# Window attention with the oldest key tile of all eight heads in a unit of its own

## The reference, cut to what matters

```python
s = jnp.einsum('bntgrd,bnsgd->bngrts', q, k).astype(jnp.float32) * scale
dist = q_pos[:, :, None] - k_pos[:, None, :]
bias = rel_bias[rel_bucket(dist)]...
valid = (dist >= 0) & (dist < WINDOW) & (k_pos[:, None, :] >= 0)     # WINDOW = 512
p = masked_softmax(s + bias[None], valid[None, :, None, None])
return jnp.einsum('bngrts,bnsgd->bntgrd', p.astype(v.dtype), v)
```

## Time and profile before

| | |
|---|---|
| median of 3 runs | 1117.7 us (1116.35 to 1119.99) |
| the profiled execution | 1116.44 us |
| its span | 1114.3 us |
| TensorE busy | 1074.0 us, 96% |
| VectorE, ScalarE, GpSimd busy | 618.8, 359.9, 88.9 us |
| mean granted TensorE clock | 0.987 |

### The profile page before, as it was taken

The page is one execution under the profiler, slowest core; times in us unless marked ns, Lnnn a source line. Parts: engine busy times, 40 slices in busy tenths (PEclk is TensorE's granted clock), DMA queues, the critical chain, the costliest instruction groups (busy, mean ns, idle before and its releaser), DMA issues.

```text
span 1114.3 us, 22552 instructions
## 1 busy us (share of the span) xinstructions
PE 1074.0 (96%) x8364; PEld 768.0 (69%) x8364; DVE 618.8 (56%) x1613; ACT 359.9 (32%) x875; POOL 88.9 (8%) x192
## 2 busy tenths in 40 slices
PE   6899999999999999998999999999999999999997
PEld 2455599998886687777876766764545476777775
DVE  0635323463423477767676666742324588888883
ACT  0422001121112475545455555631112123333330
POOL 0210100110000111100101010011000200000000
PEclk8999999999999999999999999999999999999997
DMA  9933260011006230000000000005794367788881
GB/s 350 314 114 95 79 204 2 16 35 56 1 1 123 55 106 1 1 1 1 2 1 2 1 1 1 1 1 120 162 316 150 135 220 267 268 273 290 276 216 57
DMA packets 96612, 120.25 MB, mean 108 GB/s; under 512 B 31569, under 2 KB 65380, under 8 KB 95480
## 3 DMA queue, kind: packets, MB, share of 16 engines
q1 hardware_dynamic: 96504, 118.81, 34.5%
HBM read 104.41 MB, written 14.36 MB: 107 GB/s over the span
## 4 chain that ended last, share of the span: by engine, by line
PE 84%; issue 8%; SPq 3%; DVE 3%; ACT 1%; DMA 1%; POOL 0%; ACTq 0%; POOLq 0%; DVEq 0%
PE PS L548 19%; PE PS L2047 10%; PE PS L1736 7%; PE PS L1714 7%; PE PS L1690 6%; PE PS L540 4%; PE PS L2549 3%; PE PS L1677 3%; PE PS L1711 3%; PE PS L2511 2%; PE PS L2562 2%; PE PS L1686 2%; PE PS L1242 1%; PE PS L647 1%; SPq L376 1%
## 5 line engine op out<-in xcount | busy, mean ns | idle before, releaser
L548 PE MATMUL PS<-AR 128*128 128x256 f32 (+2 forms) x896 | 219.7, 403 | 0.0
L548 PEld LDWEIGHTS PS<-AR 128*128 128x128 f32 x896 | 167.8, 190 | 45.2 <-issue 6.2
L1736 PE MATMUL PS<-CA,AR 128*128 128x128 f32 x704 | 112.2, 282 | 0.2 <-ACT AR L1790 0.2
L2047 PE MATMUL PS<-AR 128*128 128x512 f32 x256 | 112.3, 592 | 0.0
L962 DVE TENSOR_TENSOR AR<-PS,AR 128x256 f32<-128x256 f32 (+2 forms) x80 | 36.2, 453 | 134.0 <-PE PS L548 133.9
L1806 ACT ACTIVATE AR<-PS 128x512 f32<-128x512 f32 (+1 forms) x108 | 58.2, 546 | 138.6 <-PE PS L1736 137.9
L1736 PEld LDWEIGHTS PS<-CA,AR 128*128 128x128 f32 x704 | 77.9, 144 | 34.9 <-issue 25.8
L1714 PE MATMUL PS<-AR 128*128 128x65 f32 (+1 forms) x768 | 99.6, 270 | 0.0
L1714 PEld LDWEIGHTS PS<-AR 128*128 128x128 f32 x768 | 94.2, 192 | 0.2
L1790 ACT ACTIVATE AR<-PS,SM_ 128x512 f32<-128x512 f32 (+4 forms) x208 | 83.6, 475 | 17.8 <-DVE SM_ L1871 10.2
L2047 PEld LDWEIGHTS PS<-AR 128*128 128x128 f32 x256 | 47.5, 190 | 54.0 <-issue 54.0
(11 more groups left out here) (360 smaller groups left out, 1574.3 us busy)
## 6 DMA issues: line engine op xcount, KB each, us to landing
AR<-in_cache_nsa SPq DMA_DIRECT2D x128, 256.0 KB, 4.7
AR<-in_cache_mla SPq DMA_DIRECT2D x128, 96.0 KB, 3.6
AR<-in_x_prompt SPq DMA_DIRECT2D x16, 512.0 KB, 4.6
AR<-in_w_ada SPq DMA_DIRECT2D x3, 2048.0 KB, 11.8
AR<-in_w_in SPq DMA_DIRECT2D x6, 1024.0 KB, 8.7
AR<-in_w_ada SPq DMA_DIRECT2D x8, 512.0 KB, 4.4
AR<-in_w_out SPq DMA_DIRECT2D x4, 1024.0 KB, 11.4
AR<-in_w_out SPq DMA_DIRECT2D x2, 2048.0 KB, 17.5
```

The costliest lines, as they stand in the source:

```text
L548: mm = pe.matmul(bank[:, 0:WIDE[g]], tokens[:, k, :], w, start=(fresh and k == 0), stop=(last and k == 3), skip_group_check=True)
L1736: mm = pe.transpose(PS[:, 4 + c % 2, P * (t - t0):P * (t - t0) + P], tile(u, t), ident)
L2047: mm = pe.matmul(PS[0:n, 2 + 2 * (m % 2) + c, :], YTO[m % 2][:, f, 0:n], weights[:, f, 512 * c:512 * c + 512], start=(f == 0), stop=(f == 7))
```

## The change

- For each block i >= 4 a new unit `old` comes between the select and the window units. It takes one score slot (1024 columns) and holds the scores of the oldest key tile for all eight heads, 128 columns each. VectorE adds `wmask` and writes the 1024 results to `BTX[:, :, 256:384]` in SBUF, which frees the slot (`s_old`), and takes eight minima into `EM`. The unit has no exponentials and no chunks of its own.
- A window unit of blocks 4 to 7 then has four key tiles in PSUM and takes one slot. VectorE takes the minimum over the far 256 columns of both heads at once, takes the minimum of that with `EM`, and handles the nearest 256 columns per head (384 before). Its last two exponentials read `BTX` instead of PSUM. It still has ten tiles in three chunks: the first is copied by ScalarE, the second and third by VectorE, as before.
- `early` now speaks of units with exponentials, so the exponentials of a window unit stand ahead of the copies of the window unit before it.
- Window groups of block 4 are crossed and turned back too.
- The scores of a one-slot unit after a window unit with one slot wait for two exponentials of it (`MANY`, not `TWO`); after a two-slot unit they wait for all four.
- GpSimd no longer copies the mask into `BTX`.

The diff, with one line around each edit:

```diff
 NM2 = small(2)
+EM = small(8)
 NM = small(16).rearrange("p (s g) -> p s g", s=2)
...
     pool.wait_ge(s_fl, 4)
-    for h in range(H):
-        pool.tensor_copy(BTX[:, h, 256:384], wmask).then_inc(s_btw, 1)
     pool.memset(VM[:, :, :, 128:129], 2.0).then_inc(s_one, 1)
...
     nb = 1 if kind == "cmp" else i + 1 - k0
+    if kind == "win" and i >= 4:
+        UNITS.append(("old", i, 0, [(r, g) for r in range(R) for g in range(G)], k0, 1, len(GROUPS)))
     for half in range(2):
...
 for u, (kind, i, half, heads, k0, nb, og) in enumerate(UNITS):
-    if nb > 4:
+    if nb > 4 and kind != "win":
         SLOTS.append((0, 1))
...
         holds[s] = u
-    PSLOTS.append([(turn + n) % 4 for n in range(len(SLOTS[u]))])
+    PSLOTS.append([(turn + n) % 4 for n in range(0 if kind == "old" else 2 if nb > 4 else 1)])
     PPREV.append([pholds[p] for p in PSLOTS[u]])
-    turn += len(SLOTS[u])
+    turn += len(PSLOTS[u])
     for p in PSLOTS[u]:
         pholds[p] = u
-    EX0.append(EX0[u] + len(heads))
+    EX0.append(EX0[u] + (0 if kind == "old" else len(heads)))
 TWO = [len(s) == 2 for s in SLOTS]
+MANY = [unit[5] > 4 for unit in UNITS]
+OLD = [unit[0] == "old" for unit in UNITS]
+WHOLE = [u for u in range(N) if not OLD[u]]
+NTH = [sum(not old for old in OLD[:u]) for u in range(N)]
 QK0, EXP0 = [0], [0]
...
     QK0.append(QK0[u] + (2 if TWO[u] else 1))
-    EXP0.append(EXP0[u] + (4 if TWO[u] else len(UNITS[u][3])))
+    EXP0.append(EXP0[u] + (0 if OLD[u] else 4 if MANY[u] else len(UNITS[u][3])))
 QK_AT = {u: [v for v in range(N) if max(PREV[v]) == u] for u in range(-1, N)}
...
 for u, (kind, i, half, heads, k0, nb, og) in enumerate(UNITS):
-    tiles = 2 if kind == "cmp" else len(heads) * nb
+    tiles = 2 if kind == "cmp" else 0 if kind == "old" else len(heads) * nb
     CH_OF.append([])
...
 AV_LAG = 2
-TURNS_BACK = [kind in ("sel", "win") and i >= 5 for kind, i, half, last in GROUPS]
+TURNS_BACK = [kind == "sel" and i >= 5 or kind == "win" and i >= 4 for kind, i, half, last in GROUPS]
 OUT_AT = {c: [og for og, g in enumerate(GROUPS) if TURNS_BACK[og] and CH_OF[g[3]][-1] + AV_LAG + 1 == c]
...
         return 1024 * SLOTS[u][0] + 64 * gi
+    if OLD[u]:
+        return 1024 * SLOTS[u][0] + 512 * (gi % 2) + P * (gi // 2)
     return 1024 * gi if len(SLOTS[u]) == 2 else 1024 * SLOTS[u][0] + 512 * gi
...
         return EXP0[u + 1]
-    if TWO[u]:
+    if MANY[u]:
         return EXP0[u] + max(gi + (2 if n >= 4 else 0) for gi, n in map(place, range(t0, t0 + nt))) + 1
...
 
+s_old = sem("s_at_old")
 s_alone = sem("s_alone")
...
     if kind == "win" and i >= 4:
-        return [(0, k0 + 1, 4), (512, k0, 1)]
+        return [(0, k0 + 1, 4)]
     return [(P * t, k0 + t, min(4, nb - t)) for t in range(0, nb, 4)]
...
     split = before >= 0 and TWO[u] and TWO[before]
-    if before >= 0:
-        pe.wait_ge(s_exp, EXP0[before] + 2 if split else EXP0[before + 1])
+    if before >= 0 and OLD[before]:
+        pe.wait_ge(s_old, sum(OLD[:before + 1]))
+    elif before >= 0:
+        pe.wait_ge(s_exp, EXP0[before] + 2 if split or MANY[before] and not TWO[before] else EXP0[before + 1])
     if kind == "cmp":
...
                 keys = KSELT if kind == "sel" else KWINT
-                mm = pe.matmul(scores(u, gi, o, o + P * n), QT[rg, r, q], keys[rg, ks], start=True, stop=True)
+                mm = pe.matmul(scores(u, gi, o, o + P * n), QT[64 * g:64 * g + 64, r, q], keys[64 * g:64 * g + 64, ks],
+                               start=True, stop=True)
         if TWO[u] or m == len(runs) - 1:
...
         kind, i, half, heads, k0, nb, og = UNITS[u]
+        at = NTH[u] % 2
         n = 64 if kind == "cmp" else P * nb
...
                 act.wait_ge(s_trc, room_for(u, gi))
+            r, g = heads[gi]
+            sc = BTX[:, R * g + r, 256:384] if kind == "win" and lo else PSF[:, o + lo:o + hi]
             if crossed(u):
-                slot = 2 * (heads[gi][0] % 2) + heads[gi][1] + (4 if lo else 0)
+                slot = 2 * (r % 2) + g + (4 if lo else 0)
                 if og >= 4:
                     act.wait_ge(s_fin, og - 3)
-                act.activation(probs(u, gi, lo, hi), PSF[:, o + lo:o + hi], ACT.Exp, bias=NM[:, u % 2, gi:gi + 1],
+                act.activation(probs(u, gi, lo, hi), sc, ACT.Exp, bias=NM[:, at, gi:gi + 1],
                                scale=-1.0, accum_out=TOT[og % 4][:, slot:slot + 1]).then_inc(s_exp, 1)
                 continue
-            act.activation(probs(u, gi, lo, hi), PSF[:, o + lo:o + hi], ACT.Exp,
-                           bias=NM[:, u % 2, gi:gi + 1], scale=-1.0).then_inc(s_exp, 1)
+            act.activation(probs(u, gi, lo, hi), sc, ACT.Exp, bias=NM[:, at, gi:gi + 1], scale=-1.0).then_inc(s_exp, 1)
 
...
 
-    early = lambda v: v < N and len(SLOTS[v]) == 1 and len(SLOTS[v - 1]) == 1
+    early = lambda u, v: len(SLOTS[v]) == 1 and len(SLOTS[u]) == 1
     expo(0)
-    for u in range(N):
-        if early(u + 1):
-            expo(u + 1)
+    for u, v in zip(WHOLE, WHOLE[1:] + [None]):
+        if v is not None and early(u, v):
+            expo(v)
         for c in CH_OF[u]:
...
                 evac(act, c, lambda o, i: act.activation(o, i, ACT.Copy), s_evA)
-        if u + 1 < N and not early(u + 1):
-            expo(u + 1)
+        if v is not None and not early(u, v):
+            expo(v)
     for c in range(NCH, NCH + AV_LAG + 2):
...
 
+    def oldest(u):
+        _, i, half, heads, k0, nb, og = UNITS[u]
+        dve.wait_ge(s_qk, QK0[u + 1])
+        past = [v for v in WHOLE if UNITS[v][0] == "win" and UNITS[v][1] == i - 1] if i > 4 else []
+        if past:
+            dve.wait_ge(s_exp, EXP0[past[-1] + 1])
+        kept = BTX[:, :, 256:384].rearrange("p (g r) c -> p g r c", g=G)
+        dve.tensor_tensor(kept, scores(u, 0, 0, 1024).rearrange("p (g r c) -> p g r c", g=G, c=P),
+                          wmask.rearrange("p (g r c) -> p g r c", g=1, r=1).to_broadcast([P, G, R, P]), ALU.add)\
+            .then_inc(s_old, 1)
+        dve.wait_ge(s_old, sum(OLD[:u + 1]))
+        dve.tensor_reduce(EM.rearrange("p (r g) -> p g r", g=G), kept, AX, ALU.min)\
+            .then_inc(s_mx, 1)
+        far_count[0] += 1
+
     def extremes(u):
+        if OLD[u]:
+            return oldest(u)
         kind, i, half, heads, k0, nb, og = UNITS[u]
         dve.wait_ge(s_qk, QK0[u] + 1)
-        if u >= 2:
-            dve.wait_ge(s_exp, EXP0[u - 1])
-        nm = NM[:, u % 2, 0:len(heads)]
-        near = {"cmp": 64, "mla": P, "sel": min(256, P * nb),
-                "win": min(256, P * nb) if i < 4 else 384}[kind]
-        far = 0 if kind == "cmp" else P * nb - near
+        if NTH[u] >= 2:
+            dve.wait_ge(s_exp, EXP0[WHOLE[NTH[u] - 1]])
+        nm = NM[:, NTH[u] % 2, 0:len(heads)]
+        kept = kind == "win" and i >= 4
+        near = {"cmp": 64, "mla": P, "sel": min(256, P * nb), "win": min(256, P * nb)}[kind]
+        far = 0 if kind == "cmp" else P * (nb - kept) - near
         if far:
...
             dve.wait_ge(s_mx, far_count[0])
+            if kept:
+                r = heads[0][0]
+                dve.tensor_tensor(nm, nm, EM[:, 2 * r:2 * r + 2], ALU.min).then_inc(s_mx, 1)
+                far_count[0] += 1
+                dve.wait_ge(s_mx, far_count[0])
         dve.wait_ge(s_qk, QK0[u + 1])
...
             if i == 0:
-                dve.wait_ge(s_btw, 14)
+                dve.wait_ge(s_btw, 6)
             s = scores(u, 0, 0, 256).rearrange("p (r g c) -> p r g c", r=2, g=G)
...
             return
-        if kind == "win" and i == 4:
-            dve.wait_ge(s_btw, 8)
         for gi, (r, g) in enumerate(heads):
...
     for u in range(N):
-        for og in FIN_AT[CH_OF[u][0]]:
+        for og in FIN_AT[CH_OF[u][0]] if CH_OF[u] else []:
             dve_finish(dve, og)
...
     else:
-        if TURNS_BACK[og] and TWO[last]:
+        if TURNS_BACK[og] and MANY[last]:
             dve.tensor_tensor(TOT[og % 4][:, 0:4], TOT[og % 4][:, 0:4], TOT[og % 4][:, 4:8], ALU.add).then_inc(s_cl, 1)
-            dve.wait_ge(s_cl, 2 + sum(TURNS_BACK[o] and TWO[GROUPS[o][3]] for o in range(og + 1)))
+            dve.wait_ge(s_cl, 2 + sum(TURNS_BACK[o] and MANY[GROUPS[o][3]] for o in range(og + 1)))
         dve.reciprocal(RC, o[:, :, 64] if not TURNS_BACK[og] else TOT[og % 4][:, 0:4]).then_inc(s_rc, 1)
...
     gt = GAT[:, i, :].rearrange("p (g r b) -> p r g b", g=G, r=R)[:, 2 * half:2 * half + 2, :, br]
```

## The result

The changed kernel took 1119.5 us (median of 20 runs, 1117.89 to 1125.87); beside it the kernel before took 1116.5 us (median of 20, 1112.51 to 1119.99). The ratio is 1.0041, with a 95% interval of 1.0028 to 1.0054: slower by about 4.6 us (3.1 to 6.0). I had forecast +2.7. The profiled execution of after took 1121.52 us.

A forecast was written before the change was run, and what follows sets the result against it. TensorE's own queue was taken as the bound, busy 1074.0 of 1114.3 us. Terms -3.7 + 0.7 - 1.5 + 2.2 + 5.0 = +2.7 on 1117.7 gave 1120.4 us, range 1115.0 to 1124.5.

The forecast's parts named there:

- the case without a bubble: Rival: the pipeline fills while TensorE still works on the select unit, so no wait at window 1; 1115.4 us, chance 0.20.
- Removed two-slot waits: Blocks 5 to 7: TensorE's waits before window 3, window 4 and MLA 1 go, 1.24 us per block, -3.7 us.
- Same work: Blocks 4 to 7: the oldest-tile unit adds 1.05 us, four shorter window score blocks save some; +0.7 us over four blocks.
- crossing: Block 4: crossed window units save -2.2 us, turning two groups back costs +0.7, together -1.5 us.
- Stricter wait: Blocks 5 to 7: the oldest-tile unit waits for all four select exponentials, not two; 0.9, 0.66, 0.66, sum +2.2 us.
- The bubble at window 1: Blocks 4 to 7: window unit 1's third chunk waits for ScalarE's copy behind window 2's exponentials; +5.0 us.
- VectorE, 0: Blocks 4 to 7: VectorE's added addition and minimum over 1024 elements, 2.5 us per block, cost TensorE 0.
- hidden by up to 0.7: VectorE's delay of window 1's exponentials: 0.2 us late in block 5, in the other blocks hidden by up to 0.7.
- as the units of blocks 0 to 3 do now: Window units of blocks 5 to 7: one score slot each, exponentials one unit ahead, as in blocks 0 to 3; part of -3.7.
- The clock did not fall: Rival: TensorE's clock falls in the bubble, some 1.7 us per stretch in two to four blocks; 1123.8 to 1127, chance 0.12.
- The two exponentials from SBUF: Each window unit: ScalarE's last two exponentials read SBUF, 36 ns more each, within the rounding.

The follow-up runs named there:

- e13: e12 with the window groups of block 4 left uncrossed; ratio 0.9982 to the kernel before.
- e12: e10, but at the first window unit only one exponential of the next unit stands ahead of the first chunk's copy; ratio 0.9981 to the kernel before.
- e1: The kernel before with only block 4's window groups crossed and turned back; ratio 0.9996 to the kernel before.
- e5: The changed kernel with the last select unit's exponentials head by head, the oldest unit waiting for head 0's two; ratio 1.0014 to the kernel before.
- e3: The changed kernel with the first chunk's copy ahead of the next unit's exponentials at window unit 1 only; ratio 1.0016 to the kernel before.
- e9: The changed kernel with two of the next window unit's exponentials, then the first chunk's copy, then the other two; ratio 1.0005 to the kernel before.
- e8: The changed kernel with VectorE's minimum over the 1024 oldest-tile values taken twice; ratio 1.0098 to the kernel before.
- e2: The changed kernel with block 4's window groups left uncrossed as before; ratio 1.0028 to the kernel before.
- e10: e9 with the last select unit's exponentials also head by head, as in e5; ratio 0.9991 to the kernel before.
- e4: The changed kernel with the first chunk's copy ahead of the next unit's exponentials at every window unit; ratio 1.0005 to the kernel before.

## Why the prediction held, step by step

The time lies in the range and the sign was right; the size was not: +2.7 forecast, +4.6 by the runs and +5.1 by the blocks. The range was wide enough to hold the case without a bubble too, so that the time lies in it says little of the mechanism; the waits by address say more. Of the steps:

- **Removed two-slot waits, -3.7.** Two of the three went: in after the loads of window 4 (603.80) stand with the usual 0.17 and those of MLA 1 (611.16, 670.60, 735.06) with none, where the earlier trace rows has 0.29 and 0.73. The third did not quite. I had named 0.17 for window 3's loads, and they wait for window 1's exponentials, 1.02, 1.13 and 0.69 us in blocks 4 to 6:

```profile
598.24 0.30 PEld L1700 LDWEIGHTS PS<-AR 64*128 64x128 f32 x4 [1.13 <-ACT AR L1801]
```

Little of that reaches the matmuls (0.19, 0.30 and 0). By the matmuls' idleness what went is 3.1 of the 3.4 us that before has; the rest is inside what the busy time shows, as matmul ends are modelled and a load's 0.29 leaves no gap.

- **Same work, +0.7, and crossing, -1.5.** Busy time fell by 1.66 for the -0.8 of the two steps, some of it such short waits. The +0.7 was too much. In block 5 the oldest unit and window 1's scores run from 591.64 to the next piece:

```profile
593.60 1.09 PE L1747 MATMUL PS<-CA,AR 128*128 128x128 f32 x8
```

Without the 1.06 of window 1's scores that leaves 0.9 us for the oldest unit, where I had 1.05, and the term comes to about 0. The crossing's share was put too high as well: in e13 and e12, where nothing waits in it, a window unit of block 4 takes 4.30 us (545.18 to 549.48) and crossed 3.85 (545.20 to 549.05), 0.45 less and not 0.55. In e1 what was won came back as waiting (+0.17 in all), and even e12 against e13 leaves 0.3 us in the kernel, not 1.5. I had named "0 if the copies of the turned output are waited for" as a bound; what was waited for were the exponentials.
- **Stricter wait, +2.2.** 2.5 us of idleness after, 0.28 before; e5 gives back 2.4. Right, by block too (1.02, 0.60 and 0.59 more for my 0.9, 0.66 and 0.66), with the ScalarE order as its cause.
- **The bubble at window 1, +5.0.** 4.9 us, by block 0.76, 1.09, 1.57, 1.49 for my 1.0, 1.35, 1.4, 1.2. The main term was right in place, cause and size in all (e3, e9). Its neighbours were not worked out.
- **VectorE, 0.** Its pair took 2.45 us (1225 and 1222 ns) for my 2.5, window 1's second long exponential ended 6.5 us after the oldest scores began, for my 6.6, and window 3's scores came 0.30 late in block 5, where I had 0.2, and 0.19 in block 4. Small, as said, 0.5 us in all. Of my "hidden by up to 0.7" e8 finds 0.5 us in block 7, 0.1 in block 6 and nothing in block 4: a further 1.2 us cost 0.9 per block on the mean.
- **The step that failed** is the sentence that with the exponentials one unit ahead all goes "as the units of blocks 0 to 3 do now". That holds only if a step is as long on TensorE as on ScalarE. Window 3's step has no score products (the next unit, MLA 1, needs both slots), so TensorE comes to its third chunk early, and window 4's exponentials start late, as they wait for window 2's buffer. That is the wait of 0.51 in all four blocks, 2.0 us. It is as large as the whole difference between 2.7 and 4.86, but only because the other misses cancel: 0.6 of removed waits too few and 0.5 of window 3's scores on one side, 0.9 of work and 0.1 of bubble on the other. That is luck.
- **The rivals.** The bubble formed. The clock did not fall in a window stage of after; it did in one of the experiments, at 1.6 us for my 1.7. The Trainium skill (TensorE: Matmul & The Clock Gate, "What's actually happening") says that the default state is throttled and activity releases it; e5 agrees in direction, but after and e2 had the same bubble and 1.00, so it did not let me say which of the two would happen.
- **The two exponentials from SBUF.** 128 elements took 394 ns from SBUF in after and 376 from PSUM before, 18 ns more. The rows by line, before and after:

```profile
L1787 ACT ACTIVATE AR<-PS,SM_ 128x128 f32<-128x128 f32 x24 | 8.7, 376 | 0.0
L1801 ACT ACTIVATE AR<-AR,SM_ 128x128 f32<-128x128 f32 x32 | 12.4, 394 | 0.0
```

The 36 ns of the earlier trace rows lie above it; nothing hangs on it. The Trainium skill (VectorE: DVE Perf Modes, the section on the TRN2 errata) has 224 fixed cycles for SBUF and 172 for PSUM, an estimated 43 ns, which is above both.

What stays open: whether e10, e12 and e13 beat the kernel before. Their block sums are 2.8, 3.0 and 2.4 us below it and their ratios 0.999, 0.998 and 0.998, but all three intervals reach 1, so no kernel here is shown to be faster than before. Nor was it tried what sets the clock after a bubble.

## What to carry to other kernels

Where one engine's queue holds work for two consumers, moving one piece ahead can only pick which of them is late (e3, e4, e12); cutting the longer piece in two served both (e9). List, for each step, every piece that stands behind the moved one, and the next consumer of each, before a wait is counted as gone. A pipeline that runs one unit ahead has to be checked at its first unit and at every step whose work is shorter than the rest, since the steady flow shows neither. Work taken off TensorE is worth its time only while nothing waits right behind it.

## What the runs showed that I had not expected

- The same bubble (1.57 us of idleness in front of the same transposes in block 6) left the granted clock at 1.00 in two profiled executions and was followed by 0.66 in a third. I could not see from the rows which it would be.
- A VectorE operation of 1.22 us cut into four and moved into the units cost 3.1 us net: each part of 0.42 us stands in its unit's chain, and the whole had stood in front of the first unit only.
- The crossed value products are shorter one by one (16 in 1.02 us, against 8 in 0.84), and still they bought at most 0.3 us of the kernel, even where hardly anything waited behind them.
